# One modulation pair per step of the linear attention, and nine pairs moved behind it

## The reference

```python
ada_p = cp @ w_ada[l] + b_ada[l]
ada_s = cs @ w_ada[l] + b_ada[l]
...
shift1, scale1, gate1, shift2, scale2, gate2 = [a[:, None, :] for a in jnp.split(ada, 6, axis=-1)]
h = x * (1 + scale1) + shift1
...
o, s_gla_new = _gla(q, k, v, logf.reshape(B, T, GLA_HEADS, GLA_DK), s_gla)
o_gla = (_rms_norm(o, gla_norm_g) * jax.nn.silu(gg.reshape(B, T, GLA_HEADS, GLA_DV))).reshape(B, T, GLA_WIDTH)
```

## Time and profile before

| | us |
|---|---|
| median of 3 runs | 3650.65 (3647.67 to 3658.72) |
| profiled execution | 3661.24, span 3659.5 |
| TensorE busy | 3407.7 (93%) |
| VectorE busy | 1472.9 (40%) |
| ScalarE busy | 1173.5 (32%) |
| mean granted clock of TensorE | 0.956 of 2.4 GHz |
| linear attention stage, layer 0 | about 223 to 367 |
| linear attention stage, layer 1 | about 2019 to 2165.6 |

### The profile page before, as it was taken

How to read it: one execution, slowest core, us unless ns; L and a number is a source line. 1 busy time by engine, 2 the same in 40 slices (tenths; PEclk the granted TensorE clock), 3 DMA queues, 4 the chain that set the end, 5 groups by cost and what they waited for, 6 DMA issues and landing times. The chain is left out here.

```text
span 3659.5 us, 54768 instructions
## 1 busy us (share of the span) xinstructions
PE 3407.7 (93%) x22788; PEld 2935.1 (80%) x22788; DVE 1472.9 (40%) x2878; ACT 1173.5 (32%) x2210; POOL 195.2 (5%) x252
## 2 busy tenths in 40 slices
PE   6987898998999999999989868999989999999997
PEld 5864556666999999999979545666679999999997
DVE  5136665445342223232531476644445322222324
ACT  5135554444241111112321545544424211111123
POOL 0011211110000000000000121111100000000000
PEclk9997998998999999999989879999989999999998
DMA  5144102442011111111011620044310111111111
GB/s 207 29 150 143 28 1 104 162 163 80 12 41 40 48 44 44 44 49 43 22 50 29 225 89 1 1 162 162 139 47 18 47 41 52 40 48 38 50 53 50
DMA packets 93764, 255.71 MB, mean 70 GB/s; under 512 B 11548, under 2 KB 45630, under 8 KB 82631
## 3 DMA queue, kind: packets, MB, share of 16 engines
q1 hardware_dynamic: 81990, 168.24, 14.3%
q0 software_dynamic: 11520, 83.89, 6.4%
HBM read 245.59 MB, written 6.51 MB: 69 GB/s over the span
## 5 line engine op out<-in xcount | busy, mean ns | idle before, releaser
L398 PE MATMUL psum<-h_hi,w_ffn_hi 128*128 128x384 f32 (+1 forms) x2112 | 696.9, 330 | 0.4 <-DVE h_lo L2188 0.4
L400 PE MATMUL psum<-h_hi,w_ffn_lo 128*128 128x384 f32 (+1 forms) x2112 | 693.6, 328 | 0.0
L399 PE MATMUL psum<-h_lo,w_ffn_hi 128*128 128x384 f32 (+1 forms) x2112 | 683.7, 324 | 0.0
L398 PEld LDWEIGHTS psum<-h_hi,w_ffn_hi 128*128 128x128 f32 x2112 | 396.5, 188 | 1.6 <-issue 1.0
L399 PEld LDWEIGHTS psum<-h_lo,w_ffn_hi 128*128 128x128 f32 x2112 | 396.7, 188 | 0.0
L400 PEld LDWEIGHTS psum<-h_hi,w_ffn_lo 128*128 128x128 f32 x2112 | 395.7, 187 | 0.0
L398 PE MATMUL psum<-ffn_act_hi,w_ffn_hi 128*128 128x384 f32 (+1 forms) x906 | 296.0, 327 | 0.0
L400 PE MATMUL psum<-ffn_act_hi,w_ffn_lo 128*128 128x384 f32 (+1 forms) x906 | 295.8, 326 | 0.0
L399 PE MATMUL psum<-ffn_act_lo,w_ffn_hi 128*128 128x384 f32 (+1 forms) x906 | 295.5, 326 | 0.0
L384 DVE SCALAR_TENSOR_TENSOR xT<-psum,adaT,xT 128x384 f32<-128x384 f32 (+1 forms) x240 | 136.2, 572 | 384.8 <-PE psum L400 384.5
L2204 DVE TENSOR_TENSOR ffn_act<-silu_tmp,psum 128x384 f32<-128x384 f32 x132 | 70.2, 532 | 544.0 <-PE psum L400 544.0
(11 more groups left out here) (391 smaller groups left out, 5970.7 us busy)
## 6 DMA issues: line engine op xcount, KB each, us to landing
w_ada_pair<-in_w_ada SPq DMA_DIRECT2D x48, 1024.0 KB, 5.0
w_ffn<-in_w_gu SPq DMA_DIRECT2D x88, 512.0 KB, 3.5
w_ffn<-in_w_down SPq DMA_DIRECT2D x32, 384.0 KB, 3.1
w_ada_first<-in_w_ada SPq DMA_DIRECT2D x4, 2048.0 KB, 21.1
w_out<-in_w_out SPq DMA_DIRECT2D x16, 512.0 KB, 7.1
w_ffn<-in_w_down SPq DMA_DIRECT2D x22, 320.0 KB, 2.9
w_in_T<-in_w_in_T SPq DMA_DIRECT2D x12, 512.0 KB, 4.5
z<-in_x_prompt SPq DMA_DIRECT2D x8, 512.0 KB, 6.6
```

Of the source, the lines that this page charges most:

```text
L398: pe.matmul(o, wh, xh, start=first, stop=False)
L399: pe.matmul(o, wh, xl, start=False, stop=False)
L400: return pe.matmul(o, wl, xh, start=False, stop=last)
```

## The change

TensorE's steps 1 to 9 hold one pair each, pair s+6, between `cumulate` and `attend`. Nine pairs (`LATE_PAIRS`) come later: 16 to 18 in step 10 ahead of `output(8)`, 19 to 21 behind it and ahead of the turns, and 22, 23 and the last `ada_turn` between turns 2 and 3. ScalarE copies one pair per step, ahead of `blocks_of`. Its two roots become a helper: `gate_root(0)` stands ahead of the copies of pairs 16 to 20, and `gate_root(1)` behind the copy of pair 20. On VectorE the copies of the turns come ahead of `ada_vectors` instead of behind it. Loads, matmuls and copies are the same in number and size.

```diff
+            LATE_PAIRS = ((16, 17, 18), (19, 20, 21), (22, 23))
...
                         if s <= NBLK:
-                            pair_1 = 2 * s + 5
-                            pair(pair_1) if pair_1 < len(pairs) else None
+                            pair(s + 6)
                             if s == 1:
                                 pe.wait_ge(s_r, 12)
                             attend(s - 1)
-                            pair(pair_1 + 1) if pair_1 + 1 < len(pairs) else None
+                        else:
+                            for q in LATE_PAIRS[0]:
+                                pair(q)
                         if s >= 2:
                             output(s - 2)
-                    pe.wait_ge(s_ac, len(pairs))
-                    ada_turn(pe, pairs[-1]).then_inc(s_at, 1)
+                    for q in LATE_PAIRS[1]:
+                        pair(q)
                     for g in range(len(turns)):
+                        if g == 3:
+                            for q in LATE_PAIRS[2]:
+                                pair(q)
+                            pe.wait_ge(s_ac, len(pairs))
+                            ada_turn(pe, pairs[-1]).then_inc(s_at, 1)
                         pe.wait_ge(s_og, 1 if g < 4 else 2)
...
                         if s <= NBLK:
-                            for q in range(2 * s + 5, min(2 * s + 7, len(pairs))):
-                                if q % 2 == 0:
-                                    blocks_of(s - 1)
-                                kept(q)
-                            if 2 * s + 6 >= len(pairs):
-                                blocks_of(s - 1)
+                            kept(s + 6)
+                            blocks_of(s - 1)
                         recurrence(s)
-                    for i, (b0, b1) in enumerate(HALVES):
+
+                    def gate_root(i):
+                        b0, b1 = HALVES[i]
                         v = GS[:, H_GLA * b0:H_GLA * b1]
                         act.wait_ge(s_n, i + 1)
                         act.activation(v, v, ACT.Sqrt, scale=1.0 / DV, bias=EPS[:, 1:2]).then_inc(s_sq, 1)
+                    gate_root(0)
+                    for q in LATE_PAIRS[0] + LATE_PAIRS[1]:
+                        kept(q)
+                        if q == LATE_PAIRS[1][1]:
+                            gate_root(1)
+                    for q in LATE_PAIRS[2]:
+                        kept(q)
                     turned(act, act.copy, 1, s_tc)
...
                     gated(1)
+                    turned(dve, dve.tensor_copy, 0, s_td)
                     dve.wait_ge(s_at, 1)
                     ada_vectors(dve, s_av, bank(7), 48)
-                    turned(dve, dve.tensor_copy, 0, s_td)
```

## The result

The changed kernel takes 3689.97 us (median of 5 runs, 3681.19 to 3697.9) against 3658.72 us for the kernel before beside it (3647.67 to 3667.47). The ratio is 1.009 with a 95% interval of 1.0071 to 1.0109, so it is slower by 26 to 40 us. The forecast was 3678 us, slower by 27, with a range of 3660 to 3695. The profiled execution took 3690.44 us, its span 3688.6.

A forecast was written before the change was run, and what follows sets the result against it. A three-engine loop nearly bounds full-clock steps; VectorE bounds the stretch behind the recurrence. Tail 14.6 us less 1 gained in steps is 13.6 per layer, 27 for both, on 3650.65: 3678 us, range 3660 to 3695.

The forecast's parts named there:

- The tail, 14.6 us more per layer: From the end of `squares(0)` to VectorE's last copy: 15.63 us becomes 30.2, bounds 12.5 (warm) and 17 (cold) more.
- t0: The end of `squares(0)` in a layer, from which the prediction counts the times of the tail.
- the root's gate: ScalarE's copy of pair 16 stands behind `gate_root(0)`, so pair 17 cannot start before t0; `output(8)` ends at t0+12.
- the chain of loads: Tail: with two buffers, pair q+2 loads when pair q is done, 5.0 us each; pair 23's weights arrive at t0+25.2.
- The steps, 1 us gained per layer: Recurrence with one pair fewer in steps 1 to 8: gain 3.7 us, less 2.8 for one more half-clock step.
- The loop: One recurrence step through three engines, `cumulate` to the next `cumulate`: 6.96 us at full clock, 9.78 at half.
- free intervals: Times between successive masks, all but each layer's ScalarE-bound fourth and seventh; forecast as the loop, 6.96 or 9.78 us.
- one more step at half clock than before: Recurrence: the emptier TensorE loses full clock in one further step, costing 2.8 us per layer.
- clock down in every step: Rival, chance 0.20: TensorE's waits put each step at 1.2 GHz; steps lose 5.8 us per layer, 3691 us in all.
- faster: Rival, chance 0.04: the tail has room for the late pairs and costs nothing; layer gains 6.5 us, 3638 us in all.
- The stores behind the loads: Four stores on SP, issued by t0+22, cost nothing, or 2 us or so if the loads slip further.
- Mask 7 to t0, 0.4 us gained: End of the recurrence: the copy of pair 23 leaves ScalarE's queue in step 9, gain 0.4 us per layer.

The follow-up runs named there:

- another kernel: Kernel before with its pairs placed anew, and the copies of pairs 22 and 23 behind the first root: 3658.55 us, ratio 1.0025 to the kernel before.
- ten thin layers: Layers of the changed kernel and four edits of it: late pairs left out, root moved, loads left out, both last; 3689.97, 3658.84, 3665.75, 3679.86, 3664.88 us.
- the filler: Changed kernel with six idle matmuls behind `attend` in each of steps 1 to 8: 3689.42 us, ratio 1.009 to the kernel before.

## Why the prediction was right, and where it was not

- *The tail, 14.6 us more per layer.* Right: 13.94 and 15.27. In layer 0 its estimates came out as t0+12 for the end of `output(8)` (12.5), t0+16.1 for the second root (16.48), t0+18.7 for the end of `gated(1)` (19.03), t0+20 for the end of pair 21 (20.25), t0+30.2 for the end (29.57). The mechanism is shown by taking each cause away: the root's gate is worth about 11 us of the tail per layer, the loads about 3 to 4 as the tail stands and 2 with the root moved, and both together 12.7 to 12.9. Alone in another kernel the gate costs about 3 us; there only one pair stands between the root and `output(8)`, and none behind it.
- *The sizes in it.* A pair at half clock took 2.8 us (354.82 to 357.67, and 358.16 to 360.94) instead of 2.6, so `output(8)` began at t0+6.8 and not at 6.4. Right was a shorter `output(8)` than before (4.71 against the 5.72 of the earlier trace rows; I had 4.5). Pair 23's weights came just as TensorE asked (0.17 us of waiting), where I let the chain of loads set its time.
- *The steps, 1 us gained per layer.* This step failed. The changed kernel's own trace has the seven intervals 1.5 and 2.2 us longer, and over ten layers with thin steps against four of the kernel before the means are 65.6 and 63.5. The loop itself was nearly right: free intervals are 7.02 us at full clock and 10.08 with the loop's matmuls at half (forecast 6.96 and 9.78), the ScalarE-bound ones 9.59 and 11.24. What failed is the count of half-clock steps. I took "one more step at half clock than before"; the changed kernel's ten free intervals hold one at 7.03 and none of the other nine below 7.8. In ten thin layers 7 of 50 free intervals were at 7.02 or 7.03; in the kernel before, 14 of 20 (two executions) were between 7.02 and 7.27. I also took steps 1 and 2 as unchanged, and they went from 8.62 + 7.27 to 9.35 + 7.84 in layer 0 and from 7.64 + 7.65 to 10.09 + 10.08 in layer 1. The rival "clock down in every step" (a loss of 5.8) was too far the other way: with the 0.4 us behind mask 7 the loss is 1.1 and 1.9 us, or 1.7 by the ten layers.
- *The argument against that rival.* It gave TensorE 9.8 us of work in a half-clock loop of 9.78 and let the clock rise again for that. The 9.8 us are those of step 6 before, which held two pairs. With one pair TensorE is busy 8.62 of the 10.08 us from 2077.76 to 2087.84, and it waits again at the end. Nor did the clock rise at once where TensorE was busy without a break: see the last row below.
- *The number of late pairs.* The text ahead of the prediction and the prediction itself say nine. `LATE_PAIRS` holds eight, 16 to 23. At 1.43 us they are 11.4 us and not 12.9; no term of the forecast hangs on it, only the rival "faster".
- *The baseline.* I put the sum to a median of 3 runs, 3650.65. With 5 runs it was 3658.72. Of the 12 us between forecast and result 8 are this. The other 4 have the sign and about the size of what the steps lost against my 1 us of gain, which is 5 us for both layers by the changed kernel's trace.
- *The stores behind the loads.* They were issued by 377, with a median of 4.5 us to landing, so they were down before the last copy, as said.
- *Mask 7 to t0, 0.4 us gained.* Right: 24.82 to 24.44 in both layers.

The granted clock shows where the time went. These are two stretches of the changed kernel's layer 0, the end of the recurrence and the time behind t0 up to the end of `output(8)` (length, busy time of the five engines, clock, DMA share, GB/s):

```profile
330.00:352.00 22.00, 13.19 (x134) 7.44 (x133) 15.56 (x30) 13.06 (x19) 7.26 (x5) 0.50 0.30 104
354.20:366.60 12.40, 11.29 (x64) 6.24 (x64) 5.95 (x3) 1.31 (x4) 2.95 (x2) 0.60 0.50 170
```

The first is at 1.2 GHz throughout. The same stretch behind mask 7 of the kernel before had 0.66:

```profile
327.00:349.00 22.00, 16.12 (x150) 9.46 (x143) 15.16 (x30) 13.43 (x20) 6.85 (x5) 0.66 0.01 1
```

In the steps the clock can be followed too. The first row is the start of a `cumulate` on TensorE in layer 1 of the changed kernel. Below it are stretches around it: the end of the step ahead of it, the matmuls of the loop, and the end of the step. The last one is a stretch of layer 0:

```profile
2087.84 1.23 PE L781 MATMUL psum<-consts,log_forget 128*128 128x260 f32 x2 [1.46 <-DVE gla_q_blocks L1091]
```

```profile
2084.80:2087.80 3.00, 1.58 (x16) 1.03 (x16) 2.81 (x10) 1.35 (x4) 0.00 (x0) 1.00 0.60 242
2088.00:2094.20 6.20, 6.20 (x43) 3.25 (x43) 1.03 (x4) 3.44 (x9) 0.00 (x0) 0.50 0.05 10
2095.20:2097.80 2.60, 1.31 (x15) 0.76 (x14) 2.42 (x10) 1.27 (x4) 0.00 (x0) 1.00 0.58 238
...
285.60:306.00 20.40, 20.35 (x154) 11.45 (x153) 8.54 (x28) 13.41 (x28) 0.00 (x0) 0.50 0.31 104
```

The clock is up at the end of the step and during the wait of 1.46 us, falls right behind it, and comes back about when the scores are done. This is the pattern of the rival "clock down in every step". Between mask 0 and mask 7 of the ten thin layers without filler the clock fell 38 times, each time in a wait of TensorE ahead of `cumulate` or some 1.7 us at most behind its end. All 17 such waits of 2.4 us or more had a fall, and 21 of the 34 waits of 1.42 to 1.46 us. With the filler the waits of 1.46 us are gone from these steps; two waits per layer are left (1.56 and 2.67 us), and the clock fell twice per layer, 8 times in four layers. The kernel before has 10 falls in its four layers. Once down it stayed down for 3 us or more, for the whole 20.40 us of the last row with TensorE busy. So the half-clock steps that I had too few of go with the waits that the change put into the steps.

The Trainium skill ("TensorE: Matmul & The Clock Gate", section on HAM oscillation) describes bursts of matmuls between waits, each burst starting at half rate, in a loop with waits of about 3 to 5 us for a DMA. For the waits of 2.4 to 4.0 us here the traces agree (17 of 17); the waits of about 1.46 us are shorter than those of the page, and 21 of 34 had the clock fall.

What stays open is which of the short waits bring the clock down, and what ends a half-clock stretch: the same program has them in different places from one execution to the next.

## What to carry to other kernels

Work that fills another engine's gaps is free only as long as every resource it needs is free in the gap. Here the matmuls fitted into TensorE's idle time, but the copy of the first late pair stood in ScalarE's queue behind a wait of 9.4 us, and with one row buffer and one bank that stopped all that followed. Before moving a chain of small pieces, ask for each piece which queue it joins and what is waiting at the head of that queue; moving three copies ahead of one root gave back 22 to 24 of 31 us. And taking TensorE work out of a loop that other engines bound gains little: here at most 0.25 us per step at full clock (7.27 to 7.02). It turns the work into waits, and here the clock fell behind more than half of those.

## What the runs showed of the hardware

The clock of TensorE made the thin steps come in two sizes, 7.02 and 10.08 us, or between the two where it changed within a step. Which steps are the long ones changes between executions of the same kernel: the first interval of the kernel before was 8.62 us in one execution and 11.66 in the other. In the steps of the ten thin layers each of the 38 falls of the clock lay in a wait of TensorE or some 1.7 us at most behind it, the shortest of these waits being 1.42 us. A stretch of 20.40 us in which TensorE was busy for 20.35 stayed at 1.2 GHz. With idle matmuls in place of the short waits more steps stayed at full clock (10 of 20 free intervals at 7.02 or 7.03 us, against 7 of 50), but a filler that meets half clock takes 2.85 us instead of 1.56, and the time of the whole kernel showed no gain from it.
